# Five modulation sets in the first layer's attention, on two rings, with a z unit among the norms

## The reference, cut to what matters

```python
mods = jnp.einsum('bd,lde->lbe', jax.nn.silu(c), ada_w) + ada_b[:, None, :]
for i in range(DEPTH):
    sh_m, sc_m, g_m, sh_f, sc_f, g_f = jnp.split(mods[i][:, None, :].astype(x.dtype), 6, axis=-1)
    h = rms_norm(x, norm_w[i, 0]) * (1 + sc_m) + sh_m
    ...                                     # y = ab_mixer(h, ...) in layer 0
    x = x + g_m * rms_norm(y, norm_w[i, 1])
    h = rms_norm(x, norm_w[i, 2]) * (1 + sc_f) + sh_f
    x = x + g_f * rms_norm(conv_ffn(h, ...), norm_w[i, 3])

# in ab_mixer
proj = h @ w_in
z, xbc, dt_raw, q, k, v = jnp.split(proj, AB_SPLITS, axis=-1)
y_a = mamba2_ssd_mixer(z, xbc, dt_raw, conv_w, conv_b, dt_bias, a_log, d_skip, norm_w)
y_b = swa_sink_attention(q, k, v, sinks, rel_bias)
```

## Time and profile before

| | us |
|---|---|
| median of 3 runs | 1160.6 |
| lowest and highest | 1160.04, 1170.23 |
| the profiled execution | 1168.71 |
| its span | 1166.6 |
| PE busy in it | 1066.9 (91%) |
| DVE, ACT busy | 819.5, 642.6 |

### The profile page before, as it was taken

The page is one execution under the profiler, slowest core; times in us unless marked ns, Lnnn a source line. Parts: engine busy times, 40 slices in busy tenths (PEclk is TensorE's granted clock), DMA queues, the critical chain, the costliest instruction groups (busy, mean ns, idle before and its releaser), DMA issues.

```text
span 1166.6 us, 26558 instructions
## 1 busy us (share of the span) xinstructions
PE 1066.9 (91%) x9583; PEld 976.9 (84%) x9583; DVE 819.5 (70%) x1738; ACT 642.6 (55%) x1384; POOL 20.0 (2%) x11
## 2 busy tenths in 40 slices
PE   4799877969999999999999998769998999999997
PEld 4799767967789999887999986669987779999886
DVE  0587423667588888977888674687656998888844
ACT  2566625326476666447666645336745457666544
POOL 0000000000000000000000000130010000000000
PEclk9899889988999999999999998989999999999999
DMA  9657325652666555873676342021301674566562
GB/s 350 217 173 244 116 109 217 252 201 73 181 250 182 180 180 180 318 259 96 216 237 200 131 149 73 1 73 56 93 2 60 238 263 144 181 180 181 179 180 90
DMA packets 55115, 195.58 MB, mean 168 GB/s; under 512 B 6099, under 2 KB 8147, under 8 KB 54908
## 3 DMA queue, kind: packets, MB, share of 16 engines
q1 hardware_dynamic: 55036, 194.49, 50.7%
HBM read 193.39 MB, written 1.07 MB: 167 GB/s over the span
## 4 chain that ended last, share of the span: by engine, by line
PE 79%; DVE 10%; DMA 4%; ACT 3%; issue 3%; SPq 1%; DVEq 0%; ACTq 0%
PE proj L520 52%; PE acc L520 25%; DMA ada_long<-in_ada_stream 2%; DVE w_lo L1517 2%; DMA ada_ssd<-in_ada_stream 1%; DMA ada_first<-in_ada_stream 1%; SPq L422 1%; PE acc L753 1%; DVE ada_sum L1532 1%; DVE yn L1671 1%; ACT w_hi L1107 1%; DVE x L1678 1%; DVE mmat L1824 0%; DVE y_mix L1859 0%; DVE state L1985 0%
## 5 line engine op out<-in xcount | busy, mean ns | idle before, releaser
L1517 DVE TENSOR_TENSOR w_lo<-raw,w_hi 128x512 fp32r<-128x512 f32 x528 | 358.3, 684 | 112.4 <-ACT w_hi L1107 110.6
L1107 ACT ACTIVATE w_hi<-raw 128x512 fp32r<-128x512 f32 x528 | 327.6, 624 | 164.9 <-PE acc L520 127.5
L520 PE MATMUL proj<-h_hi,w_hi 128*128 128x256 f32 x1376 | 393.3, 286 | 2.5 <-DVE w_lo L1517 2.0
L520 PE MATMUL proj<-h_lo,w_hi 128*128 128x256 f32 x1376 | 391.3, 284 | 4.5 <-DVE h_lo L1725 4.4
L520 PE MATMUL proj<-h_hi,w_lo 128*128 128x256 f32 x1376 | 390.3, 284 | 0.0
L520 PEld LDWEIGHTS proj<-h_lo,w_hi 128*128 128x128 f32 x1376 | 265.2, 193 | 6.7 <-DVE h_lo L1725 6.7
L520 PEld LDWEIGHTS proj<-h_hi,w_hi 128*128 128x128 f32 x1376 | 265.2, 193 | 5.4 <-issue 2.8
L520 PEld LDWEIGHTS proj<-h_hi,w_lo 128*128 128x128 f32 x1376 | 265.1, 193 | 0.0
L520 PE MATMUL acc<-w_hi,a_hi 128*128 128x512 f32 x304 | 123.4, 406 | 4.6 <-DVE w_lo L1517 2.2
L520 PE MATMUL acc<-w_lo,a_hi 128*128 128x512 f32 x304 | 120.5, 396 | 0.0
L520 PE MATMUL acc<-w_hi,a_lo 128*128 128x512 f32 x304 | 120.0, 395 | 0.0
(11 more groups left out here) (287 smaller groups left out, 1440.5 us busy)
## 6 DMA issues: line engine op xcount, KB each, us to landing
raw<-in_w_stream SPq DMA_DIRECT2D x264, 512.0 KB, 3.6
ada_long<-in_ada_stream SPq DMA_DIRECT2D x40, 512.0 KB, 6.8
ada_ssd<-in_ada_stream SPq DMA_DIRECT2D x24, 512.0 KB, 5.5
ada_first<-in_ada_stream SPq DMA_DIRECT2D x20, 512.0 KB, 4.7
ada_out<-in_ada_stream SPq DMA_DIRECT2D x12, 512.0 KB, 5.4
hankel<-bias_scratch SPq DMA_DIRECT2D x2, 1024.0 KB, 5.9
x<-in_x_tiles SPq DMA_DIRECT2D x1, 1024.0 KB, 10.4
cst<-in_constants SPq DMA_DIRECT2D x1, 864.0 KB, 5.3
```

What stands on the lines that cost most here:

```text
L520: return pe.matmul(out, a, b, start=start, stop=stop, skip_group_check=True)
L1107: act.activation(hi, src, ACT.Copy).then_inc(w_rounded, 1)
L1517: dve.tensor_tensor(lo, src, hi.bitcast(F32), ALU.subtract).then_inc(w_split, 1)
```

## The change

Attention of layer 0 loads five sets and takes four of them, where it loaded and took three: sets 4 to 8 (units 16 to 35) are loaded there, in turn into `ada_first` (4, 6, 8) and into a new ring `ada_mid` (5, 7), which lies where `hankel0` was; so set 5 waits only for the last use of `hankel0`, set 6 for set 4 to be taken, set 7 for set 5, set 8 for set 6. Set 7 stands between the heads' values at head 3, and z0 unit 3 with the turn of set 7 at head 5. Set 8 is taken in the SSD stage's head, where 7 was. ACT copies set 4's rows after the third exponent and does z0 unit 0's step after the fifth. DVE does the stream steps of z0 units 1, 2 and 3 after the fourth norm, after the eighth and after the second result. The turns of sets 4 and 5 come one set later. In the SSD stage each z0 unit moves up by one (unit 4 in the head, 5 + n in step n, n < 7), and sets 9 to 12 stand in steps 1, 3, 5 and 7; `ada_ssd` holds units 36 to 51. Nothing is computed otherwise than before; the transfers are the same in number and size.

```diff
--- before.py
+++ after.py
@@ -57,3 +57,4 @@
 
-ADA_RINGS = {range(0, 16): 8, range(16, 28): 4, range(28, 52): 4, range(52, 72): 8, range(72, 80): 4, range(80, 92): 6, range(92, 96): 8}
+ADA_MID = (*range(20, 24), *range(28, 32))
+ADA_RINGS = {range(0, 16): 8, range(16, 36): 4, range(36, 52): 4, range(52, 72): 8, range(72, 80): 4, range(80, 92): 6, range(92, 96): 8}
 
@@ -165,2 +166,3 @@
         ada_first = sb("ada_first", [P, 4, 8, P], at=arena + 62 * KB)
+        ada_mid = sb("ada_mid", [P, 4, 8, P], at=arena + 20 * KB)
         ada_ssd = sb("ada_ssd", [P, 4, 8, P], at=at_hi)
@@ -350,6 +352,6 @@
             size = ADA_RINGS[units_]
-            ring = ada_long if size == 8 else ada_out1 if size == 6 else ada_ssd if units_[0] == 28 else ada_first
+            ring = ada_long if size == 8 else ada_out1 if size == 6 else ada_ssd if units_[0] == 36 else ada_mid if m in ADA_MID else ada_first
             return ring[:, m % size:m % size + count], size
 
-        quad_rows = lambda i: (PB[2 - i % 2] if i < 4 else PB[3])[:, P * (i % 2 + 1):P * (i % 2 + 2)]
+        quad_rows = lambda i: (PB[2 - i % 2] if i < 4 else PB[3] if i > 6 else PB[2] if i == 5 else AB[3])[:, P * (i % 2 + 1):P * (i % 2 + 2)]
         ada_group = lambda m: next(p for p, q in enumerate(ADA_GROUPS) if m in q)
@@ -416,3 +418,5 @@
                 slot, size = ada_slots(m)
-                if any(m in q and m - size in q for q in ADA_RINGS):
+                if 24 <= m < 36:
+                    sp.wait_ge(ada_rows_mm, m // 4 - 1)
+                elif any(m in q and m - size in q for q in ADA_RINGS) and not 16 <= m < 24:
                     if m - size in ADA_SUMMED:
@@ -464,3 +468,4 @@
             load_w(n_z0 + 1)
-            for k in range(2):
+            sp.wait_ge(hankel_mm, 1)
+            for k in range(4):
                 for m in range(20 + 4 * k, 24 + 4 * k):
@@ -468,10 +473,9 @@
                 load_w(n_z0 + 2 + k)
-            load_w(n_z0 + 4)
             sp.wait_ge(s_ready, 4)
-            for k in range(6):
-                for m in range(28 + 4 * k, 32 + 4 * k):
+            for k in range(4):
+                for m in range(36 + 4 * k, 40 + 4 * k):
                     load_ada(m)
-                load_w(n_z0 + 5 + 2 * k)
                 load_w(n_z0 + 6 + 2 * k)
-            stream(n_z0 + 17, n_up0 + 4)
+                load_w(n_z0 + 7 + 2 * k)
+            stream(n_z0 + 14, n_up0 + 4)
             for m in range(52, 60):
@@ -721,4 +725,6 @@
                         ada_quad(4 + i)
+                        if i:
+                            ada_turn(3 + i)
                         project("z0", some=(i,))
-                        ada_turn(4 + i)
+                    ada_turn(6)
                 else:
@@ -756,2 +762,7 @@
                         values(h - 1)
+                    if layer == 0 and h == 3:
+                        ada_quad(7)
+                    if layer == 0 and h == 5:
+                        project("z0", some=(3,))
+                        ada_turn(7)
                 values(AH - 1)
@@ -791,3 +802,3 @@
                     last.then_inc(d_item_mm, 1)
-                ada_quad(7)
+                ada_quad(8)
 
@@ -804,4 +815,4 @@
                 mm(PB[2][:, 48:72], C("ones"), S("da", 0, 24)).then_inc(d_cum_mm, 1)
-                project("z0", some=(3,))
-                ada_turn(7)
+                project("z0", some=(4,))
+                ada_turn(8)
 
@@ -820,9 +831,8 @@
                     last.then_inc(d_decay_mm, 1)
-                    if n < 8:
-                        project("z0", some=(4 + n,))
-                    if n % 2:
-                        if n < 11:
-                            ada_quad(8 + n // 2)
-                    elif n:
-                        ada_turn(7 + n // 2)
+                    if n < 7:
+                        project("z0", some=(5 + n,))
+                    if n % 2 and n < 8:
+                        ada_quad(9 + n // 2)
+                    elif n in (2, 4, 6, 8):
+                        ada_turn(8 + n // 2)
                     if n:
@@ -1261,2 +1271,6 @@
                                    accum_out=S("prob_sum", 8 + h, 1)).then_inc(s_exp, 1)
+                    if layer == 0 and h == 2:
+                        ada_copy(4)
+                    if layer == 0 and h == 4:
+                        stream("z0", copy_z, some=(0,))
                 if layer == 0:
@@ -1264,3 +1278,3 @@
                 if layer == 0:
-                    for i in range(3):
+                    for i in (1, 2):
                         ada_copy(4 + i)
@@ -1283,2 +1297,6 @@
                         attention_out(layer, h // 2 - 1)
+                    if layer == 0 and h == 4:
+                        ada_copy(7)
+                    if layer == 0 and h == 5:
+                        stream("z0", copy_z, some=(3,))
                 attention_out(layer, 3)
@@ -1322,3 +1340,3 @@
                 item(6, flat(b_tok[:, :, :]))
-                ada_copy(7)
+                ada_copy(8)
                 for b in range(NB):
@@ -1327,3 +1345,3 @@
                 act.activation(S("tail", 0, 24), S("tail", 0, 24), ACT.Exp).then_inc(d_tail, 1)
-                stream("z0", copy_z, some=(3,))
+                stream("z0", copy_z, some=(4,))
                 for g in range(SSD_G):
@@ -1336,6 +1354,6 @@
                     act.activation(flat(lmat[:, n % 2]), flat(lmat[:, n % 2]), ACT.Exp).then_inc(d_decay, 1)
-                    if n < 8:
-                        stream("z0", copy_z, some=(4 + n,))
-                    if n % 2 and n < 11:
-                        ada_copy(8 + n // 2)
+                    if n < 7:
+                        stream("z0", copy_z, some=(5 + n,))
+                    if n % 2 and n < 8:
+                        ada_copy(9 + n // 2)
                 silu_z()
@@ -1751,3 +1769,3 @@
                 if layer == 0:
-                    stream("z0", some=(0, 1, 2))
+                    stream("z0", some=(0,))
                 else:
@@ -1761,2 +1779,4 @@
                     dve.tensor_scalar(scores[:, h, SEQ:384], scores[:, h, SEQ:384], S("inv_sum", 8 + h, 1), None, ALU.mult).then_inc(s_norm, 1)
+                    if layer == 0 and h in (3, 7):
+                        stream("z0", some=(1 + h // 4,))
                 for t in range(4):
@@ -1764,2 +1784,4 @@
                     dve.tensor_tensor(a_lo[:, 18 + t], O_BANK[t % 2][:, 0:SEQ], a_hi[:, 18 + t].bitcast(F32), ALU.subtract).then_inc(s_ready, 1)
+                    if layer == 0 and t == 1:
+                        stream("z0", some=(3,))
 
@@ -1804,3 +1826,3 @@
                 dve.wait_ge(d_item, 9)
-                stream("z0", some=(3,))
+                stream("z0", some=(4,))
 
@@ -1838,4 +1860,4 @@
                 for n in range(12):
-                    if n < 8:
-                        stream("z0", some=(4 + n,))
+                    if n < 7:
+                        stream("z0", some=(5 + n,))
                     if n < 11:
```

## The result

| | us |
|---|---|
| before, median of 4 runs | 1161.78 (1160.04 to 1170.23) |
| after, median of 4 runs | 1188.8 (1187.62 to 1189.86) |
| ratio | 1.0218, 95% interval 1.0166 to 1.0269 |
| the profiled execution after, its span | 1189.53, 1187.4 |

What follows compares the result with a forecast made beforehand. PE's order was taken to bound the kernel, with time to win only where PE waits. Stalls 23.9 plus clock 3.3 minus gains 11.4 gave +15.8 on 1160.6, rounded to 1176.5 us; range 1162 to 1190.

Steps and rivals of the forecast that it cites:

- rival 3: "More is lost": slow clock costs 14 us instead of 3.3, attention gains 3 instead of 6.7; +30, 1191 us; chance 12%.
- Gain in attention: Attention of layer 0: sets 5 and 6 cost no wait, the end moves from 175.1 to 168.4; 6.7 us gained.
- Gain in the SSD head: SSD head: set 8, landed long before, replaces set 7, so the 3.44 us wait goes; 4.7 us gained.
- Three stalls: SSD loop, steps 1, 3 and 5: ACT wants a z0 unit queued behind a waiting set; 8.0, 8.8 and 7.1 us lost.
- T: SSD loop: the end of the set in an odd step, when SP starts to issue the next loads.
- all three timed cases show 9 or more: SSD loop, argument against rival 1's early landing: the weight unit behind a set's four units takes 9 us or more.
- The clock: SSD loop: slow clock after PE's idling, 1.4 us for two stalls and 0.5 for the third; 3.3 us, bounds 0 and 14.
- my upper bound of 4.6 each: SSD loop: the clock's cost per stall if all 6.4 us of work ran at the slow pace.
- The set that leaves step 9 gains nothing: SSD loop's end: the set ended at 251.0, before PE's next wait, which the weights end; no gain counted.
- One of the signs: SSD loop, expected in the profile after: SP's set loads 18 to 21 us apart.
- loads still run ahead: Rival 1, SSD loop: no stalls and only the 11.4 us of gains remain; 1149 us, chance 6%.
- Half a stall: Rival 2, SSD loop: the unit lands at T + 5.4, each stall is 3.7 us shorter; +1.4, 1162 us; chance 12%.

Runs made afterwards that it cites:

- the kernel with the lead: The changed kernel with only SP's SSD load order edited, z0 units loaded two units earlier (6 to 9 follow set 9): 1157.99 us, 0.9938 of before.
- the norms in one place: Against the kernel with the lead: DVE does z0 units 0, 1 and 2 ahead of the norms, as before the change; 1160.27 us, 0.995 of before.

## Why the prediction was right in its mechanism and short in its size

The forecast was 1176.5 us in a range of 1162 to 1190, and 1188.8 was measured, near its upper end and just above the 1168 to 1187 that I gave 66%. It lies inside by luck as much as by the mechanism: the range went up to 1190 for a part of rival 3, whose loss of attention's gain didn't come. Of the 12.3 us between forecast and result 1.2 are the median before, 1161.78 with its fourth run. Step by step, on the ruler:

- **Gain in attention, 6.7 foreseen: 5.9 measured** (42.9 to 37.0). Set 5 had landed, set 6 cost no wait, and the next limit was the landing of unit 4: first values foreseen at 152.1, or 19.9 after set 4's start; they stood at 20.5. The late load of set 5 takes 6.2 away and the norms in one place 2.9; each was taken away alone, and together they are more than the gain, so they aren't parts that add up. What I called fixed, 11.3 us from the values to the end and 5.0 for what is put between, was 16.5.
- **Gain in the SSD head, 4.7 foreseen:** set 8 ran in 1.95 us without a wait. Both gains together reach step 1 as 11.0 us against 11.4, so the head gave 5.1. The kernel with the lead confirms the sum once more, 11.7 at the outputs of step 6.
- **Three stalls, 8.0 + 8.8 + 7.1 = 23.9 foreseen.** The chain is the one described, ACT's three waits, each with PE's two behind it; in the first, unit at T + 9.1, turn after T + 10.7, `mmat` at T + 13.4 are the foreseen times to 0.1 us. The second and third units landed at T + 10.0 and T + 10.2, after SP had taken 3.04 and 2.98 us to issue the four units of the set in place of 1.75: 2.0 us in all. That "all three timed cases show 9 or more" was rounded: the third, 229.24 to 238.21, is 8.97.
- **The clock, 3.3 foreseen: 7.0 in the loop and 2.2 in its end.** This is the step that failed. I took one set's 1.4 us as the price of a stall. What runs slow is all that stands behind the stall until the clock is back: in after, the rows from 209.39 to 214.66, outputs, decay matmuls and nearly half of the unit. The second idle time of 1.99 us lies right ahead of them. The first two stalls cost 2.5 and 2.8 us by it, over half of my upper bound of 4.6 each, and the third 1.7 (6.45 from `mmat` to the outputs of step 6, where 4.7 was foreseen). Filling the idle time gave 6.6 of the 7.0 back.
- **"The set that leaves step 9 gains nothing"** was half the thought. The sum put nothing down for the loop's end, which ran at 0.61 in place of 0.77, and nothing for the set's landing: with the lead restored, set 12 in step 7 waits 2.76 us. The 2.2 us are in the loop's end and go with its clock, but they are not this set's as far as the runs show: the same end without the set also ran at 0.82 in 28.9 us.

The sum: 23.9 + 2.0 + 7.0 + 2.2 - 11.0 = 24.1, against 24.2 on the ruler, and 15.8 foreseen (23.9 + 3.3 - 11.4). Of the 8.3 missing, 5.9 are the clock, 2.0 the landings, 0.4 the gains.

**One of the signs failed with it.** SP's set loads were to be 18 to 21 us apart; they were 22.4 and 23.5. The others held: attention's last `a_lo` ended at 170.0, ACT waited 11.4, 14.0 and 14.5 us for `raw`, and each time PE idled before a turn and before `mmat`.

**The rivals.** That loads still run ahead (1149) is what the kernel with the lead does, and even that gains 0.6% and not the 1% of the rival, 9.3 us on the ruler against 11.4; the kernel as changed doesn't run ahead. Half a stall would have needed a landing at T + 5.4; the earliest in after was T + 9.1. "More is lost" (1191) is nearest in time, but of its two parts the slow clock came true only in part (9.2 of 14 us), and the loss of attention's gain didn't.

A waiting loop running on a slow clock is what the Trainium skill describes in "TensorE: Matmul & The Clock Gate", HAM oscillation: when a short burst of matmuls is followed each time by a wait for a transfer, every burst starts cold. The trace agrees, with 2.08 us in place of 1.16 for the decay matmuls behind each stall; the remedies that the page gives are to restructure the loop or to pad the short dimension, and the runs show that matmuls without a use do it too, 30.8 to 26.0 us.

## What to carry to other kernels

When work is shifted by a step, write down for each load what stands ahead of it on the issuing queue and when that may go; a load behind a load that waits for a ring has lost its lead, however many slots of its own are free. Price a stall as its length plus the slow clock over everything behind it until the clock is back, and give a waiting stretch a range: the same one took 28.9 and 30.8 us here. A part that looks bad as a whole can hold a good one: here the five sets and two rings gain 11 us up to the loop's end and 9 with it, and SP's order cost 33.5 (160.6 - 127.1).
